# A different order of work in the tail of each mixer group: outputs scaled beside the key factors, masked copies ahead of reciprocals and roots, exponentials first

## The reference, cut to what matters

```python
# per token: r, k, v, decay w, a (a sigmoid), kk = k * k_k, and then
kk = kk / maximum(sqrt(sum(kk * kk)), 1e-12)
k = k * (1 + (a - 1) * k_a)
S = S * w - (S kk) (kk * a)^T + v k^T;   y = S r
# the outputs are normalised per head, and a bonus is added:
y = (y - mu) * rsqrt(var + LNX_EPS) * lnx_w + lnx_b
out = (y + sum(r * k * r_k) * v) * g
# the gate: u, v = gelu(h);  v = LayerNorm(v);  out = u * (causal mix of v over 128 tokens)
```

## Time and profile before

| what | us |
|---|---|
| median of 3 runs | 3037.82 (3035.6 to 3041.42) |
| the profiled execution, its own time | 3039.42 |
| its span, first to last instruction | 3037.6 |
| the mixer in it | 609 to 1127, 518 long |
| TensorE busy in the mixer | 452.6, at a mean granted clock of 0.96 |
| VectorE, ScalarE, POOL busy in the mixer | 345.5, 250.9, 225.2 |

### The profile page before, as it was taken

One profiled execution on the slowest core, in us unless ns is written; L12 is line 12 of the kernel. 1 busy time (PEld: TensorE's weight loads), 2 busy tenths in 40 slices (PEclk: granted clock), 3 DMA queues, 4 the chain that ended last, 5 costly groups with the idle time before them and its releaser, 6 DMA issues.

```text
span 3037.6 us, 56487 instructions
## 1 busy us (share of the span) xinstructions
PE 2920.4 (96%) x23786; PEld 2496.3 (82%) x23786; DVE 1620.6 (53%) x2059; ACT 1028.5 (34%) x1804; POOL 1438.8 (47%) x993
## 2 busy tenths in 40 slices
PE   8999999988888889999999999999999999999998
PEld 7888888788888878988788888787898788888887
DVE  7331644266666662335866664545232976664452
ACT  4122211245445442334333332332232533332222
POOL 4554454343544536237545452545626654443354
PEclk9999999989999999999999999999999999999999
DMA  4433454421122213111333336454111233335632
GB/s 165 170 99 110 154 169 144 138 58 50 46 62 62 63 53 101 36 49 49 111 111 139 139 111 253 177 194 159 49 43 48 77 112 125 139 125 209 241 146 84
DMA packets 175989, 346.86 MB, mean 114 GB/s; under 512 B 47232, under 2 KB 104576, under 8 KB 170112
## 3 DMA queue, kind: packets, MB, share of 16 engines
q1 hardware_dynamic: 175744, 343.35, 33.3%
HBM read 240.53 MB, written 102.76 MB: 113 GB/s over the span
## 4 chain that ended last, share of the span: by engine, by line
PE 44%; DVE 3%; DMA 2%; issue 1%; POOL 1%; ACT 1%; SPq 0%; DVEq 0%; ACTq 0%; POOLq 0%
PE ps L2195 29%; PE ps L1658 12%; PE ps L2147 3%; DMA hidden<-hid 1%; DMA w_raw<-in_weights 1%; DMA scr<-hidden_raw 0%; DVE normed L3094 0%; POOL w_lo L806 0%; DVE t_raw L2788 0%; DVE normed L3120 0%; POOL sumsq L826 0%; PE ps L2353 0%; DVE t_raw L2796 0%; POOL sq L824 0%; DVE rstd L2365 0%
## 5 line engine op out<-in xcount | busy, mean ns | idle before, releaser
L806 POOL TENSOR_TENSOR w_lo<-w_raw,w_hi 128x512 fp32r<-128x512 f32 x256 | 383.9, 1522 | 503.0 <-ACT w_hi L1095 499.2
L1658 PE MATMUL ps<-a_hi,w_hi 128*128 128x512 f32 x1140 | 446.6, 392 | 16.0 <-DVE a_lo L2375 9.8
L1658 PE MATMUL ps<-a_lo,w_hi 128*128 128x512 f32 x1140 | 444.4, 390 | 0.0
L1095 ACT ACTIVATE w_hi<-w_raw 128x512 fp32r<-128x512 f32 x252 | 144.8, 623 | 653.6 <-PE ps L1658 518.8
L1658 PE MATMUL ps<-a_hi,w_lo 128*128 128x512 f32 x1140 | 351.4, 390 | 0.0
L2195 PE MATMUL ps<-a_hi,w_hi 128*128 128x512 f32 x800 | 313.3, 392 | 11.9 <-ACT u_t L1479 4.8
L2195 PE MATMUL ps<-a_lo,w_hi 128*128 128x512 f32 x800 | 312.1, 390 | 0.0
L2195 PE MATMUL ps<-a_hi,w_lo 128*128 128x512 f32 x800 | 311.8, 390 | 0.0
L1658 PEld LDWEIGHTS ps<-a_hi,w_hi 128*128 128x128 f32 x1140 | 214.5, 188 | 63.3 <-DVE a_lo L2375 9.8
L1658 PEld LDWEIGHTS ps<-a_hi,w_lo 128*128 128x128 f32 x1140 | 214.3, 188 | 44.9
L1658 PEld LDWEIGHTS ps<-a_lo,w_hi 128*128 128x128 f32 x1140 | 214.6, 188 | 44.1 <-issue 0.2
(11 more groups left out here) (364 smaller groups left out, 6408.2 us busy)
## 6 DMA issues: line engine op xcount, KB each, us to landing
w_raw<-in_weights SPq DMA_DIRECT2D x228, 512.0 KB, 4.0
hidden<-hid SPq DMA_DIRECT2D x44, 1024.0 KB, 3.8
zT<-z_out SPq DMA_DIRECT2D x44, 512.0 KB, 3.8
a_hi<-hidden SPq DMA_DIRECT2D x44, 512.0 KB, 8.3
a_lo<-hidden SPq DMA_DIRECT2D x44, 512.0 KB, 9.3
w_raw<-kvw SPq DMA_DIRECT2D x32, 512.0 KB, 3.2
suv<-zT SPq DMA_DIRECT2D x16, 512.0 KB, 4.5
x<-in_xT SPq DMA_DIRECT2D x16, 512.0 KB, 5.7
```

The source lines that it names most:

```text
L806: pool.tensor_tensor(low_t[:, u, part, :], w_raw[:, u, part, :], high[:, u, part, :].bitcast(F32), ALU.subtract).then_inc(S["w_lo_done"], 1)
L1095: act.activation(split_into(pair)[0][:, u, part, :], w_raw[:, u, part, :], ACT.Copy).then_inc(S["w_hi_done"], 1)
L1658: mm = pe.matmul(to[:, nb, 0:w], wt[:, u, k, :], r[:, k, nb * w:(nb + 1) * w], start=(k == 0 and r is hi_in and wt is w_hi), stop=(k == kn ...
```

## The change

Only the order inside the bodies is changed. On TensorE `cross` of level 2 goes ahead of `key_norms` and `variance`, and `scale_back` ahead of `cross` of level 4. On ScalarE the copies of level 2 go ahead of `roots`, `exps` directly behind `deviation`, and `mixing` behind the values' copy. On VectorE `reciprocals` is cut in three (`bounded`: the maximum and the gate's reciprocal; `reciprocals`: the keys' reciprocal; `gate_hat`: `v_hat`) and level 2 goes between the first two, `v_hat` behind the deviation. POOL works in the order rates, scaled query, gate, key factor, scaled key, query product, and then the bonus. No instruction, wait or buffer is added or taken away.

```diff
--- before.py
+++ after.py
@@ -961,15 +961,17 @@
                     finish(k - 1, 1 - par)
                 if scores:
                     gated(k + 1, 1 - par)
+                if ahead:
+                    n = k + 2
+                    rates(n)
+                    scaled_query(n, par)
+                    gate_norm(n)
+                    key_mixed(n, par)
+                    scaled_key(n)
+                    key_query(n, par)
+                if scores:
                     bonus_in(k + 1, 1 - par)
                 if ahead:
-                    n = k + 2
-                    key_mixed(n, par)
-                    key_query(n, par)
-                    rates(n)
-                    scaled_key(n)
-                    scaled_query(n, par)
-                    gate_norm(n)
                     pool.wait_ge(S["kt_done"], n + 1)
                     pool.wait_ge(S["rr_done"], n + 1)
 
@@ -1288,18 +1290,21 @@
                     token_major(b, k_tok[1 - par], "ktr", "ktc", 2)
                 if ahead:
                     lora_tanh(n)
+                if scores:
+                    evac_x(b, 2)
+                if ahead:
                     roots(n)
                 if state:
                     deviation(k)
-                if scores:
-                    evac_x(b, 2)
                 if ahead:
-                    mixing(n)
                     exps(n, par)
                 if scores:
                     evac_x(b, 3)
                     gates(b, 1 - par)
                     token_major(b, v_tok[1 - par], "vtr", "vtc", 6)
+                if ahead:
+                    mixing(n)
+                if scores:
                     token_major(b, b_tok[1 - par], "btr", "btc", 3)
                     evac_x(b, 4)
 
@@ -2028,11 +2033,13 @@
                     turn(b, kt, "kt_done", (S["sg_mx"], b + 1), 2, "ktr")
                 if ahead:
                     loras(n, par)
+                if behind:
+                    cross(b, q, 2)
+                if ahead:
                     key_norms(n)
                 if state:
                     variance(k)
                 if behind:
-                    cross(b, q, 2)
                     bonus_sums(b, q)
                     merge(b, q, 2)
                     lora_g(b, q)
@@ -2042,11 +2049,10 @@
                     turn(b, bt, "bt_done", (S["sg_vh"], min(b + 2, GROUPS)), 3, "btr")
                 if ahead:
                     key_scales(n)
-                if behind:
-                    cross(b, q, 4)
                 if state:
                     scale_back(k, behind)
                 if behind:
+                    cross(b, q, 4)
                     merge(b, q, 4)
 
             for pair in range(Q_IN1, Q_TAIL):
@@ -2541,14 +2547,18 @@
 
             def reciprocals(n):
 
+                dve.wait_ge(S["kn_mx"], n + 1)
+                if n:
+                    dve.wait_ge(S["kb_ps"], n)
+                dve.reciprocal(n8[:, 1, :], n8[:, 0, :]).then_inc(S["kn_rc"], 1)
+
+            def bounded(n):
                 dve.wait_ge(S["kn_rt"], n + 1)
                 dve.tensor_scalar(n8[:, 0, :], n8[:, 0, :], 1e-12, None, ALU.max).then_inc(S["kn_mx"], 1)
                 dve.wait_ge(S["sg_rt"], n + 1)
                 dve.reciprocal(bn[:, 9:10], bn[:, 8:9]).then_inc(S["sg_rc"], 1)
-                dve.wait_ge(S["kn_mx"], n + 1)
-                if n:
-                    dve.wait_ge(S["kb_ps"], n)
-                dve.reciprocal(n8[:, 1, :], n8[:, 0, :]).then_inc(S["kn_rc"], 1)
+
+            def gate_hat(n):
                 dve.wait_ge(S["sg_rc"], n + 1)
                 if n:
                     dve.wait_ge(S["sg_lw"], n)
@@ -2622,11 +2632,16 @@
                 if ahead:
                     gate_stats(n)
                     sum_decays(n)
+                    bounded(n)
+                if scores:
+                    take_level(b, q, 2)
+                if ahead:
                     reciprocals(n)
                 if state:
                     deviation(k, first)
+                if ahead:
+                    gate_hat(n)
                 if scores:
-                    take_level(b, q, 2)
                     bonuses(b, q)
                     take_level(b, q, 3)
                 if ahead:
@@ -2659,7 +2674,9 @@
                         dve.wait_ge(S["fold_st1"], FOLDED)
                         sum_decays(0)
                         gate_stats(0)
+                        bounded(0)
                         reciprocals(0)
+                        gate_hat(0)
                     elif pair == FIRST_AHEAD:
                         keys_normed(0, False)
                 if pair == Q_IN1:
```

## The result

The changed kernel takes 2999.59 us (median of 4, 2999.2 to 3003.5), against 3038.11 us (median of 4) for the kernel before, measured beside it: ratio 0.9875, 95% interval 0.9858 to 0.9893. That is 38.5 us, 1.3% less. The forecast was 3001, with 2993 to 3016 around it. The profiled execution took 2999.77 us, its span is 2998.0. Of all runs behind this document three took several thousand microseconds (5198 and 11321 with the kernel before, 6385 with the kernel that has the copies behind the roots); they are disturbed and left out of every median and ratio.

A forecast was written before the change was run, and what follows sets the result against it. Two things set a period: cross 3's start and TensorE's work from it to the scale-back. Fourteen bodies at 2.52 us plus 1.4 for first and last give 36.7 off 3039.42: 3002.7, as median 3001, range 2993 to 3016.

The forecast's parts named there:

- Cross 2, the copies, merge 2: Level 2: cross 2 takes the key norms' place, copies go ahead of the roots, merge 2 starts 0.60 us earlier.
- Cross 3: TensorE: cross 3 starts at 885.35 instead of 886.82, gain so far 1.47 us, its 0.87 us wait for VectorE gone.
- Scale-back: TensorE: scale-back at 889.78 instead of 892.30, gain 2.52 us: 1.47 and the 1.05 of cross 4.
- Scores: TensorE: next scores start at 895.22 instead of 897.74, VectorE's chain from the scale-back to them taking 5.44 us.
- the bound of 1.27 for one turn: VectorE's queries wait between 0 and 1.27 us for one POOL operation; 0.63 before, taken as no change.
- What is late next: TensorE's work ahead of the scores ends at 894.90, so their 2.01 us idle time shrinks to 0.3.
- First and last body: Mixer loop's first and last bodies each gain part of 2.52 us, taken as 0.7 each.
- ScalarE and POOL costed at nothing: The new orders on ScalarE and POOL deliver in time, POOL's scaled key included; POOL's part costed at nothing.
- The first (only the scale-back counts, 3023): Late roots leave cross 3 where it was; gain 14.7 us, 3023; chance 0.15, including gains between it and the forecast.
- The second (POOL's phase): Queries meet a whole POOL operation, 3010, or the other way 2997; within the forecast's chance of 0.75.
- The third (scaled key too late): POOL's scaled key, sixth instead of fourth, delays the key scores; 28 us more, 3066; slower, chance 0.05.
- The fourth: No change: a wait behind the scores, tied to POOL's or SP's clock, absorbs all; 3038, chance 0.05.

The follow-up runs named there:

- the kernel with POOL's wait: Changed kernel with one wait added on POOL: the scaled key waits until VectorE has made bt; 2985.32 us, ratio 0.9824.
- mixing first: Changed kernel with mixing put back ahead of the exponentials on ScalarE; 3018.92 us, ratio 0.9921 to the kernel before.

## Why the prediction was right, and where it was off

- **Cross 2, the copies, merge 2.** Forecast 2.77 us from cross 2 to merge 2, measured 2.72 (861.95 to 864.67). Undone on ScalarE it costs 0.49 a period; that is near the 0.60 of the sum only by chance, as merge 2 comes 1.31 later and the queries win 0.81 back.
- **Cross 3.** Forecast 4.97 behind cross 2, measured 4.86, with no wait.
- **Scale-back.** Forecast 9.40 behind cross 2, measured 9.18. The wait of the keys for it remains, shorter, as said: 0.78 us.
- **Scores.** Forecast 14.84 behind cross 2, measured 14.84. That it is exact is luck, since two misses cancel: 0.2 us up to the scale-back, and from it to the scores 5.66 instead of 5.44, as queries wait for POOL's key factor for longer (1.49 us instead of 1.18). The runs in which they meet no POOL operation give 0.68 for them, so they waited 0.50 before, not 0.63, and 0.81 now, inside the bound of 1.27 for one turn. The forecast had queries start 11.43 us behind cross 2 and the key factor end at 11.77; measured are 11.12 and 12.06. The short period fell by 2.51 where 2.52 was forecast.
- **What is late next: wrong.** I gave TensorE 0.3 us to spare before the scores; it has 1.30. I had read the 1.69 us from cross 4 to merge 4 as including ScalarE's copy. It was TensorE's own work, cross 4 (1.05) and the scale-back (0.64) that stood between them; with that moved, merge 4 follows cross 4 after 1.03 us (871.68 to 872.71). So the forecast's lower end, 2997, was no limit of TensorE: the kernel with POOL's wait takes 1.07 us more out of each period and ends at 2985.
- **First and last body.** Forecast 0.7 each. The first period fell from 29.16 to 27.30, 1.86. From the last tanh to the first product behind the mixer it was 53.96 and is 49.39 (1038.10 to 1087.49): 4.57, of which 2.5 is the last full tail and 2.1 belongs to the last body. There cross 2 no longer stands behind the variance, which waits for ScalarE.
- **The account of the profiled executions.** 13 periods at 2.51 make 32.6; the first 1.9; the last tail and body 4.6; over and above the short period these 13 had 5.7 us before and have 4.1 after, 1.6. Together 40.7, less 1.4 by which the first tanh is later (0.7 of it before the mixer starts), 39.3; the spans differ by 39.6.
- **The clock: missing.** Before, five periods lost 0.8 us each at a granted clock of 0.95; after, none does. It is worth a few microseconds here. With the copies behind the roots it makes nearly all of the loss (38.7 us in the profiled execution), with mixing first about 9 of 19 us, with POOL's old order about 6 of 40.
- **ScalarE and POOL costed at nothing.** In the new order they are not in the way, which is what the sum needed: right. But the text gave them no share in the gain, and they have one. With the old orders of both the changed kernel takes 22 us more; with POOL's alone 40, with mixing's alone 19. The earlier tail needs the rates and the scaled query earlier; the prediction checked that the new order was in time and did not ask whether the old one would have been.
- **The rivals.** The first (only the scale-back counts, 3023) was the time of that move alone, and not of the whole. VectorE waits 0.29 us for the roots, and TensorE does not notice. The second (POOL's phase) is real in kind: queries wait 0.3 longer. The reversals show its size: a shift of 0.2 to 1.3 us on another engine moved the queries' wait by between -0.8 and +0.2. The third (scaled key too late) did not occur: the scaled key ends at 875.69, 2.7 us before the key scores at 878.38. The fourth is out.

On taking turns the runs say more than the rows before did. With POOL held back, bt takes 0.68; with POOL busy, 1.75 in every period of the changed kernel. By the Trainium skill, "SBUF — State Buffer", Who interferes with whom, the loser waits for the whole instruction of the other; with bt as the loser the trace agrees: 1.07 us lost, and it ends 0.54 us after POOL's scaled key does (876.23 against 875.69).

## What to carry to other kernels

Measure a chain across engines by distances between starts in one period, forecast each link, and check for every engine that takes part both that its new order is in time and that its old one would not have been. When reading a distance, name what stands in it: a gap that is filled with the work about to be moved is not a wait. Do the same with a reversal: three here (mixing first, copies behind the roots, cross 2 behind the key norms) came near the expected total or period, by other links than the expected ones. And look for VectorE operations with two inputs in SBUF that sit on the critical chain beside a busy POOL: one wait, put where POOL's next result is not yet needed, gave 14 us here.

## What the hardware showed that was not expected

TensorE's granted clock falls to 1.2 GHz in some periods of a loop that is otherwise dense, and the waits in the loop do not tell in which. With merge 2 waiting 1.25 us in every group (copies behind the roots), six periods kept 2.4 GHz and 29.56 us, and six had a fall that began 0.9 to 2.1 us behind the start of merge 2, lasted 10 to 17 us and made them 34 to 37 us long. With mixing first two periods of 14 had one. These falls began 0.4 and 1.1 us behind TensorE's wait of 0.67 us for `h_st`, 13 to 14 us behind merge 3 and its wait of 1.06. The kernel before is idle for 2.01 us ahead of the scores in every period and has short falls there in five. With both old orders (1.06 before merge 3 and 1.51 before the scores) and with the moves of level 2 alone (1.06 and 1.68) no period had one. So a single idle time does not decide it; what does, and why six groups and not all, is open.

Open as well is what makes some periods 0.4 to 1.3 us longer at full clock. TensorE has gaps there for which the profile shows no wait ("issue"). In the 13 profiled executions of this study there are 64 such gaps of over 0.3 us between 630 and 1090 us. Each ends 2.2 to 2.9 us after the start of a transfer on the queue that the profile calls instruction, which starts one about every 5 us; and both executions of the changed kernel have them in the 6th, the 8th and the 14th period. Late loading of instructions would fit this; it is not shown, since no run here changed it.
